# Dilated attention on one core: the scores of two heads, on the two halves of the rows, issued one behind the other in every second unit

## The reference

```python
DIL_GROUPS = ((128, 1), (512, 4), (2048, 16))     # window, dilation
s = einsum('bdhnqe,bdhnke->bdhnqk', qs, kb) * (Dh ** -0.5) + bias      # Dh = 64
p = exp(where(valid, s, NEG_INF) - m);  denom = p.sum(-1)
o = einsum('bdhnqk,bdhnke->bdhnqe', p, vb) / denom
lse = m + log(denom)
# the groups are weighted by a softmax over lse, gated by silu(gate), projected
```

## Time and profile before

| | |
|---|---|
| median of three runs | 4429.48 us (4422.3 to 4454.76) |
| profiled execution | 4451.4 us, of which 4449.6 us span |
| granted clock, mean of the profiled execution | 0.958 |
| PE busy | 4183.7 us, 94% of the span |
| DVE, ACT, POOL busy | 1957.9, 1384.3, 1417.9 us |
| steps of group 0, 1, 2 of the dilated attention | from 153 to 318, 398 to 581, 661 to 798 us |

### The profile page before, as it was taken

The page is one execution under the profiler, slowest core; times in us unless marked ns, Lnnn a source line. Parts: engine busy times, 40 slices in busy tenths (PEclk is TensorE's granted clock), DMA queues, the critical chain, the costliest instruction groups (busy, mean ns, idle before and its releaser), DMA issues.

```text
span 4449.6 us, 50121 instructions
## 1 busy us (share of the span) xinstructions
PE 4183.7 (94%) x19671; PEld 3346.5 (75%) x19671; DVE 1957.9 (44%) x3435; ACT 1384.3 (31%) x2896; POOL 1417.9 (32%) x1449
## 2 busy tenths in 40 slices
PE   8999999789999998998888999998998988999998
PEld 4677788677888877885576888887884576888887
DVE  2231313382777765216734343445315734334444
ACT  1121212122666662214533221223214533221122
POOL 1313121181333325322134443342422133443441
PEclk9999999799999999997898999999997898999999
DMA  5312110332000003110022111113110022111112
GB/s 181 98 46 74 51 52 31 101 112 55 9 10 8 8 14 105 55 36 1 1 97 80 49 53 48 43 57 105 56 31 8 1 88 82 57 48 44 52 53 97
DMA packets 224534, 244.60 MB, mean 55 GB/s; under 512 B 43861, under 2 KB 165221, under 8 KB 224297
## 3 DMA queue, kind: packets, MB, share of 16 engines
q1 hardware_dynamic: 190456, 162.81, 12.4%
q10 hardware_dynamic: 33840, 78.58, 5.2%
HBM read 209.11 MB, written 30.08 MB: 54 GB/s over the span
## 4 chain that ended last, share of the span: by engine, by line
PE 76%; DVE 14%; ACT 5%; issue 2%; POOL 1%; DMA 1%; SPq 0%; ACTq 0%; DVEq 0%; POOLq 0%
PE ps L127 73%; PE ps L130 4%; DVE cst_sm L150 3%; DVE ml_p L139 2%; ACT thi L133 1%; DVE tlo L139 1%; DVE tfi L147 1%; DVE m_hb L147 1%; ACT m_junk L133 1%; ACT tfi L133 0%; POOL mix_z L139 0%; ACT ml_o L133 0%; ACT f_ta L133 0%; DVE m_z L147 0%; DVE m_z L139 0%
## 5 line engine op out<-in xcount | busy, mean ns | idle before, releaser
L136 POOL CAST whi<-wst 128x512 fp32r<-128x512 f32 (+3 forms) x538 | 378.2, 703 | 2065.8 <-DMA wst<-in_w_down 539.3
L139 POOL TENSOR_TENSOR wlo<-wst,whi 128x512 fp32r<-128x512 f32 (+3 forms) x538 | 704.6, 1310 | 43.2
L127 PE MATMUL ps<-thi,whi 128*128 128x512 f32 x1760 | 690.4, 392 | 8.6 <-POOL wlo L139 5.7
L127 PE MATMUL ps<-tlo,whi 128*128 128x512 f32 x1760 | 688.8, 391 | 0.0
L127 PE MATMUL ps<-thi,wlo 128*128 128x512 f32 x1760 | 688.5, 391 | 0.0
L127 PE MATMUL ps<-whi,thi 128*128 128x512 f32 (+3 forms) x1560 | 605.1, 388 | 6.0 <-DVE mix_z L139 2.6
L127 PE MATMUL ps<-wlo,thi 128*128 128x512 f32 (+3 forms) x1560 | 593.2, 380 | 0.0
L127 PE MATMUL ps<-whi,tlo 128*128 128x512 f32 (+3 forms) x1560 | 592.9, 380 | 0.0
L147 DVE SCALAR_TENSOR_TENSOR f_ta<-f_ua,tfi,f_ta 128x1024 f32<-128x1024 f32 x88 | 122.0, 1386 | 735.4 <-ACT f_ta L133 733.8
L127 PEld LDWEIGHTS ps<-thi,whi 128*128 128x128 f32 x1760 | 333.4, 189 | 79.7 <-POOL wlo L139 6.9
L127 PEld LDWEIGHTS ps<-thi,wlo 128*128 128x128 f32 x1760 | 332.9, 189 | 69.8
(11 more groups left out here) (299 smaller groups left out, 6659.9 us busy)
## 6 DMA issues: line engine op xcount, KB each, us to landing
wst<-in_w_up SPq DMA_DIRECT2D x704, 64.0 KB, 2.0
wst<-in_w_down SPq DMA_DIRECT2D x88, 256.0 KB, 2.6
wst<-in_w_in SPq DMA_DIRECT2D x64, 256.0 KB, 2.7
wst<-in_a_w_in SPq DMA_DIRECT2D x72, 192.0 KB, 2.4
wst<-in_ada_w SPq DMA_DIRECT2D x48, 256.0 KB, 3.4
tfi<-in_ada_w SPq DMA_DIRECT2D x48, 256.0 KB, 2.7
wst<-in_w_out SPq DMA_DIRECT2D x32, 256.0 KB, 5.4
m_xr<-scr_x ACTq DMA_DIRECT2D x16, 512.0 KB, 3.6
```

The lines of the kernel that those rows point to most:

```text
L127: return self.none if self.e is None else self.e.matmul(*a, **k)
L136: return self.none if self.e is None else self.e.tensor_copy(*a)
L139: return self.none if self.e is None else self.e.tensor_tensor(*a)
```

## The change

At an even step the kernel now issues the scores of unit `i` and of unit `i + 1`, head `2m` and head `2m + 1`, on rows 0 to 63 and 64 to 127, into the two banks of the ring; at an odd step it issues none. Everything else in the loop stays at its place, and the queues of the other engines are the same, row for row.

```diff
         for i in range(48 + 4):
-            if i < 48:
-                j, h = i // 6, i % 6
+            for u in (i, i + 1) if i < 48 and i % 2 == 0 else ():
+                j, h = u // 6, u % 6
                 k0, w, _, _ = geometry(g, j)
                 p = slice(64 * (h % 2), 64 * (h % 2) + 64)
-                key = ("as", g, i)
+                key = ("as", g, u)
                 b = B.take(key, "s3")
                 for event in B.freed(key):
                     q.wait_ge(*event)
```

## The result

In the first comparison the changed kernel took 4411.15 us (median of six runs, 4395.44 to 4412.9), the kernel before 4432.83 (six runs, 4422.3 to 4454.76): a ratio of 0.9937, 95% interval 0.9918 to 0.9957, 21.7 us less. Two later comparisons of the same two kernels gave 0.9905 (0.9884 to 0.9925) and 0.9916 (0.9890 to 0.9942). Over all 21 executions of the changed kernel the median is 4401.5, over all 58 of the one before 4439.3: 37.8 us or 0.85% less. The profiled execution took 4395.44, of which 4393.6 span.

A forecast was written before the change was run, and what follows sets the result against it. PE was taken to bound the groups nearly alone; 24.2 us net from the steps plus 8.1 from overlap minus 1.7 for waits gave 30.6 off 4429.5, so 4399 us, range 4380 to 4425.

The forecast's parts named there:

- What bounds: In the three groups' loops, PE sets the pace of 457 us nearly alone; the distance between its starts counts.
- The odd step loses 0.76, 0.65 and 0.56: Without scores, PE's odd step shortens by these us at 256, 192 and 128 columns.
- The second score pays its columns, 0.43 at 256: In even steps on PE, the second score adds only column time: 0.43, 0.32 or 0.21 us.
- What the other half of the rows gives: 8.1 us: Second score's first pass runs beside the first score's second; 8.1 us saved, bounds nothing and 11.8.
- nearly free: Rival: both passes of the even step's second score hidden, 23.7 us of addition falls away; 4383 us, chance 0.08.
- The sign that I had named for an even step: At 256 columns, last dense matmul to first product: 1.44 us if a pass is hidden, 1.65 if not.
- The wait that is added: 1.7 us: Second score waits for DVE behind its reciprocal; 0.34 us charged at each of at most five places.
- The clock: Clock drop at group 2's end may vanish, 9 us less, or reach other groups' ends, up to 18 more; nothing taken.
- my signs of being wrong: DVE waits in most pairs, or the clock's row below 1.00 before a group's last query block.
- The sum: Over the kernel, 24.2 + 8.1 - 1.7 = 30.6 us saved, giving 4399 us from the median of 4429.5.

The follow-up runs named there:

- fourth trace: The changed kernel run once more, unaltered, for another trace: 4401.54 us, with 445.5 us in the three groups.
- the fifth: The changed kernel run once more, unaltered, for another trace: 4400.77 us, with 446.2 us in the three groups.
- copy first: Changed kernel with DVE's gate instructions one unit later and ACT's copy of the even unit before its exponential: 4381.66 us, ratio 0.9872 to the kernel before.

## Why the prediction was right, and where it was wrong

- *What bounds.* Right: the groups are PE's, and what left PE's queue left the groups. With a busy share that was already 98% the gain was in the starts.
- *The odd step loses 0.76, 0.65 and 0.56.* Right: 0.45 measured for 0.46. The 63 pairs of steps that don't wait got shorter by 0.76, 0.65 and 0.57 at the median, first scores to first scores.
- *The second score pays its columns, 0.43 at 256.* Right for a neighbour on the same rows: 1.06 - 0.63 = 0.43 with both on one half.
- *What the other half of the rows gives: 8.1 us.* Mis-sized, and this is the step that failed: I let the second score's first pass run beside the first score's second pass at best, and bounded the term by 11.8. Both passes and both weight loads run beside the first score's, and the term is the whole 23.7 that I had worked out for the rival "nearly free", wherever the second score doesn't wait: in 63 of 72 pairs. The sign that I had named for an even step, 1.44 with a hidden pass, came out as 1.23. I had held against that rival that the second pass has no partner left; it has one, because the two scores start together.
- *The wait that is added: 1.7 us.* The mechanism and the places were right: DVE's reciprocal, units 37 and 43 of the groups. Four waits came, the longest 1.90. The size was low. With a free second score the 72 pairs should win 30 x 0.76 + 18 x 0.65 + 24 x 0.56 = 47.9 us. The last four pairs of group 2 went from 27.7 to 20.3 us, 5 more than their share, mostly since the clock was at 0.50 there before and now for the most part at 1.00. Of these 53, 46.3 arrived, so the waits cost about 7, four times the 1.7. The nine pairs whose second score starts late show the same: they got 0.7 us longer in all, where 6.1 less were due.
- *The clock.* The drop at the end of group 2 went nearly away, and one came in group 0: after the wait of 1.90 at 289 the clock was 0.50 from 292 to 295. In the fourth trace no drop followed the same wait, in the fifth it lasted to the end of the group. Neither end of my bound was reached. One of my signs of being wrong did come, a row below 1.00 before the last query block of a group: in group 2, behind the wait at step 38 (0.51 from 732 to 734). The kernel before has its drop in the same block, so this sign was badly chosen and tells nothing of the change.
- *The sum.* 30.6 us were forecast and 21.7, 43.6 and 37.7 measured in three comparisons, 37.8 over all runs. The time of the first comparison, 4411, is 12 above the forecast, the 4401.5 over all runs 3 above. Against the groups, 46.3, the sum was low by the 15.6 of the overlap and the 5 of the clock, and high by the 5 of the waits; and 8 to 9 of the 46.3 don't show in the medians. That the time over all runs came within 3 us of the forecast is in part luck: these errors went against each other.
- *Where the rest is.* The six traces of the changed kernel hold 442.6 to 446.2 in the groups, 43 to 46 less than before, and the medians over all runs differ by 38. A part of the spread is shown: the first layer of differential attention takes 280 or 291 us in either kernel. The second took 313.9 and 307.0 in the two traces of the kernel before and 303.5 to 303.7 in all six of the changed one; whether the change has a part in that is open. That the executions of 4405 to 4413 us, which none of the traces caught, are of that kind, I have not shown; a drop of the clock at PE's new waits in untraced executions would fit too. For the latter speaks that the version without them (copy first) stayed within 6 us in five runs, the changed kernel within 28 in 21.

## What to carry to other kernels

In this kernel a matmul on half of the rows cost twice: its own columns, and some 0.34 us for the queue's way from 128 rows to 64 and back. With two of them on different halves and in different banks, right behind each other, the second was free, float32 passes included; with transposes and products of 128 rows between them almost nothing was left of that (5.55 us a pair for 5.57). Where you can place two such neighbours, look at who must have emptied the second one's bank: its wait now stands a step earlier, and a long instruction on the emptying engine, here a reciprocal, should be moved out of that interval.

## What the runs showed of the hardware

Two float32 matmuls on different halves of the rows, neighbours in the queue and with nothing to wait for, start 0.007 us apart, in both of their passes. The Trainium skill, "TensorE: Matmul & The Clock Gate", Part 3 on packing small matmuls, has distinct row groups start some 4 ns apart, which is near the 5 to 8 ns of the 63 pairs here, and matmuls strictly in program order in start and end. Read of whole matmuls, as one score ahead of the other, the trace agrees (424.110 and 424.117). Read of passes, as the prediction did, it doesn't: the second score's first pass at 424.117 starts 0.31 before the first score's second at 424.431. The measurement decides.

The overlap is not tied to like matmuls: a score on the upper half started between two passes of a product on the lower half (421.92 and 422.07 above). And where the second score had to wait for its bank, its passes followed at their own time and the pair cost two full scores, with the transposes behind (728.49 and 730.22 above).
